# A scale moved behind the second layer's input projections

## The chip, the cores and the metric

One of the eight cores of a Trainium2 chip. The metric is the device time of one execution, in microseconds (us), and the number quoted is the median of repeated executions. Engines: TensorE (PE, with its weight loads shown apart as PEld), VectorE (DVE), ScalarE (ACT), GpSimd (POOL), and SyncE (SP), which issues the weight DMAs.

## The reference

Two transformer layers on 256 tokens (plus 16 meta tokens in the first), width 1024, in fp32. What surrounds the change is the end of layer 1 and the start of layer 2:

```python
        h = h + (jax.nn.silu(a @ w_gate[i]) * (a @ w_up[i])) @ w_down[i]

    h = rmsnorm(h, final_norm)
    return h[:, N_META:N_META + s_len]
...
    h = x
    for i in range(DEPTH):
        u = rms_norm(h, norm1_g[i])
        p_rwkv, p_nsa = jnp.split(u @ w_in[i], [N_RWKV_COLS], axis=-1)
        y_rwkv = rwkv7_time_mix(p_rwkv, ...)
        y_nsa = nsa_attention(p_nsa, ...)
```

So two norms follow each other with nothing between them: y = h * rsqrt(mean(h^2) + eps) * g3, and u = y * rsqrt(mean(y^2) + eps) * g4. Then 25 tiles of 128 projected features are made from u, of which 14 also get the time shift p + mu * (p_prev - p) before they are used.

## The kernel before

Activations lie feature-major: 8 tiles (k = 0 to 7) of 128 features by 256 tokens. Every fp32 product of activations with weights is made from three fp32r products: the operands are split into a rounded part (`hi`, by ACT) and a rest (`lo`, by DVE), and `part_products` (L536, matmuls on L539 to L541) adds hi*hi, hi*lo and lo*hi. Weights come in blocks of two tiles (1 MB) into a ring of two; for tile t, ACT's `split_hi` (L1382) writes `w_hi` and DVE's `split_lo` (L1851) writes `w_lo`, into 4 slots. `split_hi(t + 4)` can't start before tile t has been used up.

Each engine runs its own list of instructions in order, written out by hand; semaphores order them against each other (`wait_ge(name, n)` waits until the n-th instruction that signals the name is done).

**The end of layer 1.** The last two of the 22 down products run together, so that the 8 output tiles f come ready one after the other (`last_downs`). `add_down` (L2106) adds each to the residual `res`.

**The two norms.** With r = 1/sqrt(mean(h^2) + eps), both norms together scale a token by one factor, 1/sqrt(mean((g3^2 + eps) h^2) + eps^2). ACT squares each residual tile times sqrt(g3^2 + eps) (L1601), PE sums over features with 8 products with a matrix of ones into bank 3 (L864, fp32, each recorded as two passes), ACT makes the root (L1611, L1612), and DVE writes `act_in = res * (g3 g4) * root` (L2123), which ACT rounds (L1391) and DVE subtracts (L1859). Only then does tile 0 of the projections start. The plain squares, for r, are made by ACT (L1605) and summed by 8 further products in bank 2 (L869): five before tile 0, three between its products. r scales the residual later, off the path (L2200).

**The 25 projections.** PE's loop (from L980) makes tile t in bank t % 2: 24 matmuls. Before tile t it waits for the split of its weights and for tile t - 2 to have been read. Between the tiles PE does the small products of the two mixers: `decay_and_rate` before tile 3, `gates` before tile 4, `turn_values` before 6 and 12, key sums before 14 and 16, and for each of 8 attention units u: `nsa_scores` before tile 7 + 2u, `nsa_turn` (L960) before 10 + 2u and `nsa_values` (L975) before 11 + 2u.

A tile is read as follows. Plain tiles (2 to 10, 23, 24): ACT copies it out of the bank (L1680, L1682), and signals `proj2_plain`. Shifted tiles (0, 1 and 11 to 22): ACT writes mu * tile into `shift_buf` (L1677), and DVE adds the rest (L2182), and signals `shifted`. In its iteration t ACT then does `split_hi(t + 4)`, and, for odd t, the exponentials of unit (t - 7) / 2 (L1647) and the copy of the turned weights of unit (t - 9) / 2 (L1655), which `nsa_values` waits for. DVE in its iteration t does `split_lo(t + 4)`, for even t `nsa_kept` (L2160 to L2170) and `nsa_maxima` (L2150), and single steps such as L2200 (t = 5, 7, 9, 11), the key sums (13, 15), L2211 (15), L2215 and L2218 (17), L2221 and L2225 (19).

Layer 1's projections (L1968) read each tile with one DVE instruction that also scales it.

Of the kernel before, what the change touches and what calls it, by code (L numbers as in the profile page):

```python
# [13 lines left out]
P = 128  # L14
# [7 lines left out]
D = 1024  # L22
# [156 lines left out]
def constant_tables():  # L179
# [5 lines left out]
    c["eps_twice"] = np.full((P, 1), EPS * EPS)  # L185
# [82 lines left out]
def build_program(nc, xT, weights, consts, vecs, out):  # L268
# [14 lines left out]
    with ctx:  # L283
# [11 lines left out]
        gain_eps = sb("gain_eps", [P, KT])  # L295
# [42 lines left out]
        sq_gained = flat[:, 0:KT * SEQ].rearrange("p (k t) -> p k t", k=KT)  # L338
        sq_plain = flat[:, KT * SEQ:2 * KT * SEQ].rearrange("p (k t) -> p k t", k=KT)
# [195 lines left out]
        def _(pe):  # L535
# [326 lines left out]
            for k in range(KT):  # L862
                pe.wait_ge(S("norm_squares"), (nth("norm3") - 1) * KT + k + 1)
                mm = pe.matmul(ps[:, 3, 0:SEQ], C("ones"), sq_gained[:, k, :], start=(k == 0), stop=(k == KT - 1))  # L864
            mm.then_inc(S("norm_sums"), 1)

            def plain_sum(k):
                pe.wait_ge(S("plain_squares"), k + 1)
                mm = pe.matmul(ps[:, 2, 0:SEQ], C("ones"), sq_plain[:, k, :], start=(k == 0), stop=(k == KT - 1),  # L869
                               skip_group_check=True)  # L870
                if k == KT - 1:
                    mm.then_inc(S("plain_sums"), 1)

            for k in range(5):
                plain_sum(k)

# [103 lines left out]
            for t in range(TILES2):  # L980
                if t == 3:
                    decay_and_rate()
                if t == 4:
                    gates()
# [20 lines left out]
                if t >= 2:  # L1005
                    if is_shifted(t - 2):
                        pe.wait_ge(S("shifted"), shifted_upto(t - 2))
                    else:
                        pe.wait_ge(S("proj2_plain"), plain_upto(t - 2))
                if t == 0:  # L1010

                    for k in range(KT):
                        pe.wait_ge(S("normed"), normed("norm4", k))
                        mm = part_products(ps[:, 0, 0:SEQ], T_IN2 % SLOTS, k, act_hi[:, k, 0:SEQ], act_lo[:, k, 0:SEQ],
                                           k == 0, k == KT - 1)
                        if k == KT - 1:
                            mm.then_inc(S("proj2_ready"), 1)
                        if 2 <= k < 5:
                            plain_sum(k + 3)
                else:  # L1020
                    tile_products(ps[:, t % 2, 0:SEQ], (T_IN2 + t) % SLOTS, SEQ).then_inc(S("proj2_ready"), 1)
# [41 lines left out]
            pe.wait_ge(S("proj2_plain"), plain_upto(TILES2 - 1))  # L1063
# [286 lines left out]
        def _(act):  # L1350
# [245 lines left out]
            act.wait_ge(S("gains_squared"), 1)  # L1596
            step(act.activation(gain_eps[:], gain_eps[:], ACT.Ln, bias=C("eps")))
            step(act.activation(gain_eps[:], gain_eps[:], ACT.Exp, scale=0.5))
# [5 lines left out]
            def plain_square(k):  # L1604
                act.activation(sq_plain[:, k, :], res[:, k, META:CTX], ACT.Square).then_inc(S("plain_squares"), 1)  # L1605

            split_hi(T_IN2 + SLOTS - 2)
            for k in range(5):
                plain_square(k)
            act.wait_ge(S("norm_sums"), nth("norm3"))  # L1610
            step(act.activation(nrm[:, 0, 0:SEQ], ps[:, 3, 0:SEQ], ACT.Ln, bias=C("eps_twice"), scale=1.0 / D))  # L1611
            act.activation(nrm[:, 0, 0:SEQ], nrm[:, 0, 0:SEQ], ACT.Exp, scale=-0.5).then_inc(S("norm_root"), 1)  # L1612
            split_hi(T_IN2 + SLOTS - 1)
            for k in range(KT):
                round_tiles(0, SEQ, act_in, (k,))
                if k < 3:
                    plain_square(5 + k)
            act.wait_ge(S("plain_sums"), 1)
            step(act.activation(nrm[:, 1, 0:SEQ], ps[:, 2, 0:SEQ], ACT.Ln, bias=C("eps"), scale=1.0 / D))
            act.activation(nrm[:, 1, 0:SEQ], nrm[:, 1, 0:SEQ], ACT.Exp, scale=-0.5).then_inc(S("norm3_root"), 1)  # L1620
# [9 lines left out]
            def gather_blocks(x):  # L1630
                act.wait_ge(S("proj2_plain"), plain_upto((KC0, VC0)[x]))
# [39 lines left out]
            for t in range(TILES2):  # L1671
                act.wait_ge(S("proj2_ready"), t + 1)
                if is_shifted(t):
                    k = shifted_upto(t) - 1
                    if k >= 2:
                        act.wait_ge(S("shifted"), k - 1)
                    act.activation(shift_buf[:, k % 2, 1:1 + SEQ], ps[:, t % 2, 0:SEQ], ACT.Copy, scale=V("mu", k))\  # L1677
                        .then_inc(S("shift_scaled"), 1)
                elif t == GL0:
                    act.activation(proj2[0:24, t, :], ps[0:24, t % 2, 0:SEQ], ACT.Sigmoid).then_inc(S("proj2_plain"), 1)  # L1680
                else:
                    act.activation(proj2[:, t, :], ps[:, t % 2, 0:SEQ], ACT.Copy,  # L1682
                                   scale=HD ** -0.5 if Q0 <= t < Q0 + 4 else 1.0).then_inc(S("proj2_plain"), 1)
# [9 lines left out]
                if t == 2:  # L1693
# [6 lines left out]
                if t == 3:  # L1700
# [143 lines left out]
        def _(dve):  # L1844
# [258 lines left out]
            def add_down(layer, t):  # L2103
# [7 lines left out]
            dve.tensor_tensor(gain34[:], V("norm3", 0, KT), V("norm4", 0, KT), ALU.mult)  # L2111
            dve.tensor_tensor(gain_eps[:], V("norm3", 0, KT), V("norm3", 0, KT), ALU.mult)\
                .then_inc(S("gains_squared"), 1)
            for t in range(KT):
                add_down(1, t)


            split_lo(T_IN2 + SLOTS - 2)
            split_lo(T_IN2 + SLOTS - 1)
            dve.wait_ge(S("norm_root"), nth("norm3"))  # L2120
            for k in range(KT + 1):
                if k < KT:
                    dve.scalar_tensor_tensor(act_in[:, k, 0:SEQ], res[:, k, META:CTX], gain34[:, k:k + 1],  # L2123
                                             nrm[:, 0, 0:SEQ], ALU.mult, ALU.mult).then_inc(S("act_full"), 1)
                if k > 0:
                    rest("norm4", k - 1, SEQ, act_in)

# [50 lines left out]
            for t in range(TILES2):  # L2178
                if is_shifted(t):
                    k = shifted_upto(t) - 1  # L2180
                    dve.wait_ge(S("shift_scaled"), k + 1)
                    dve.scalar_tensor_tensor(proj2[:, t, :], ps[:, t % 2, 0:SEQ], om_mu[:, k:k + 1],  # L2182
                                             shift_buf[:, k % 2, 0:SEQ], ALU.mult, ALU.add).then_inc(S("shifted"), 1)
                if t + SLOTS < TILES2:
                    split_lo(T_IN2 + t + SLOTS)

                if t == 3:
# [360 lines left out]
```

## Time and profile before

| what | value |
|---|---|
| device time, median of 3 | 769.53 us (768.79 to 775.48) |
| the profiled execution: its own time | 774.36 us |
| its span (first to last record) | 772.6 us |
| its mean granted TensorE clock | 0.985 of full |
| busy: PE, DVE, ACT | 743.2, 503.7, 414.4 us |
| last down product of layer 1 starts | 351.11 us |
| tile 0 and tile 1 of the second projections start | 359.46, 365.42 us |
| first product behind the projections starts | 464.10 us |

A row of the timeline says when an instruction started, how long it took, and in brackets how long its engine sat idle before it and whose end released it. Rows can stand for several instructions in a row (xN). Consecutive instructions of one engine overlap a little, so that the distance between two starts is the cost in a queue, and the duration is what a waiting engine sees. Of the records of a matmul some are missing now and then.

### The profile page before, as it was taken

The numbers are of one execution on the slowest core, as the hardware profiler recorded it, in microseconds if no ns is written. First come the engines' busy times: TensorE is split into PE (matmuls) and PEld (weight loads), VectorE is DVE, ScalarE is ACT, GpSimd is POOL, SyncE is SP. The second block draws the span as 40 slices with busy tenths as digits, with TensorE's granted clock in tenths as the row PEclk, the third lists the DMA queues.
The fourth block names the chain that finished last, engine by engine and source line by source line (L and its number), as shares of the span: only waits on it lengthen the run. The fifth ranks groups of instructions, "written<-read, shape, count | busy, mean of one in ns | idle before, by whom it ended". The sixth has DMA issues, their size and how long they took to land.

```text
span 772.6 us, 16370 instructions
## 1 busy us (share of the span) xinstructions
PE 743.2 (96%) x6606; PEld 671.8 (87%) x6606; DVE 503.7 (65%) x913; ACT 414.4 (54%) x734; POOL 5.6 (1%) x13
## 2 busy tenths in 40 slices
PE   6999998999999999998999999989999999999996
PEld 5878786998888889997999998888898888889995
DVE  4655454668899994446566865444478999996445
ACT  5544544475666664337786662223367666665332
POOL 0000000000000000001000000000000000000000
PEclk9999999999999999999999999989999999999999
DMA  6622231336666454543343332301144645455431
GB/s 225 223 101 99 76 109 61 108 127 250 222 245 217 170 210 169 195 179 109 110 165 109 110 111 110 112 3 58 56 165 164 218 164 207 173 197 184 176 149 55
DMA packets 16740, 113.82 MB, mean 147 GB/s; under 512 B 2000, under 2 KB 2128, under 8 KB 3632
## 3 DMA queue, kind: packets, MB, share of 16 engines
q1 hardware_dynamic: 15984, 109.22, 39.7%
q0 software_dynamic: 704, 3.85, 1.5%
q8 instruction: 40, 0.66, 0.4%
q14 instruction: 12, 0.10, 0.0%
HBM read 112.01 MB, written 1.05 MB: 146 GB/s over the span
## 4 chain that ended last, share of the span: by engine, by line
PE 91%; DVE 4%; ACT 3%; issue 1%; DMA 1%; SPq 0%; DVEq 0%
PE ps L554 21%; PE ps L539 13%; PE ps L541 12%; PE ps L540 12%; PE ps L556 11%; PE ps L893 6%; PE ps L975 2%; DVE w_lo L1851 1%; PE ps L1031 1%; PE ps L855 1%; PE ps L721 1%; PE ps L960 1%; ACT w_hi L1382 1%; DMA vec<-in_vecs 1%; PE ps L933 0%
## 5 line engine op out<-in xcount | busy, mean ns | idle before, releaser
L1851 DVE TENSOR_TENSOR w_lo<-ring,w_hi 128x1024 fp32r<-128x1024 f32 x194 | 237.1, 1223 | 126.8 <-ACT w_hi L1382 125.6
L1382 ACT ACTIVATE w_hi<-ring 128x1024 fp32r<-128x1024 f32 x194 | 204.0, 1054 | 121.5 <-PE ps L541 110.7
L554 PE MATMUL ps<-acts,w_hi 128*128 128x512 f32 x704 | 246.2, 393 | 0.0
L556 PE MATMUL ps<-acts,w_lo 128*128 128x256 f32 x704 | 197.5, 281 | 0.0
L554 PEld LDWEIGHTS ps<-acts,w_hi 128*128 128x128 f32 x704 | 132.2, 188 | 29.5
L539 PE MATMUL ps<-acts,w_hi 128*128 128x256 f32 (+1 forms) x464 | 140.4, 303 | 6.2 <-DVE acts L1859 2.5
L541 PE MATMUL ps<-acts,w_lo 128*128 128x256 f32 (+1 forms) x464 | 133.7, 288 | 0.0
L540 PE MATMUL ps<-acts,w_hi 128*128 128x256 f32 (+1 forms) x464 | 133.6, 288 | 0.0
L556 PEld LDWEIGHTS ps<-acts,w_lo 128*128 128x128 f32 x704 | 132.4, 188 | 0.1
L539 PEld LDWEIGHTS ps<-acts,w_hi 128*128 128x128 f32 x464 | 89.5, 193 | 13.8 <-issue 7.3
L541 PE MATMUL ps<-hid_hi,w_lo 128*128 (+1 forms) x352 | 99.7, 283 | 0.0
L539 PE MATMUL ps<-hid_hi,w_hi 128*128 (+1 forms) x352 | 99.7, 283 | 0.0
L540 PE MATMUL ps<-hid_lo,w_hi 128*128 (+1 forms) x352 | 99.7, 283 | 0.0
L540 PEld LDWEIGHTS ps<-acts,w_hi 128*128 128x128 f32 x464 | 89.6, 193 | 1.2 <-issue 1.0
L541 PEld LDWEIGHTS ps<-acts,w_lo 128*128 128x128 f32 x464 | 89.6, 193 | 0.0
L539 PEld LDWEIGHTS ps<-hid_hi,w_hi 128*128 128x128 f32 x352 | 67.6, 192 | 0.1
L541 PEld LDWEIGHTS ps<-hid_hi,w_lo 128*128 128x128 f32 x352 | 67.6, 192 | 0.0
L540 PEld LDWEIGHTS ps<-hid_lo,w_hi 128*128 128x128 f32 x352 | 67.6, 192 | 0.0
L1968 DVE SCALAR_TENSOR_TENSOR arena<-ps,nrm 128x272 f32<-128x272 f32 (+1 forms) x21 | 9.1, 436 | 37.3 <-PE ps L541 37.3
L1574 ACT ACTIVATE hid_hi<-f 128x256 f32 (+1 forms) x44 | 18.4, 419 | 27.5 <-DVE f L2078 27.5
L1567 ACT ACTIVATE yT<-ps 128x256 f32<-128x256 f32 x44 | 16.6, 378 | 26.1 <-PE ps L556 26.0
L1562 ACT ACTIVATE yT<-ps 128x256 f32<-128x256 f32 x44 | 16.7, 379 | 21.2 <-PE ps L556 21.0
(344 smaller groups left out, 921.8 us busy)
## 6 DMA issues: line engine op xcount, KB each, us to landing
ring<-in_weights SPq DMA_DIRECT2D x101, 1024.0 KB, 4.8
res<-in_xT SPq DMA_DIRECT2D x2, 544.0 KB, 4.2
ring<-in_weights SPq DMA_DIRECT2D x2, 512.0 KB, 4.8
cst<-in_consts POOLq DMA_DIRECT2D x1, 1024.0 KB, 5.2
out_features<-yT SPq DMA_DIRECT2D x4, 256.0 KB, 2.2
cst<-in_consts POOLq DMA_DIRECT2D x1, 945.5 KB, 4.9
vec<-in_vecs POOLq DMA_DIRECT2D x1, 677.0 KB, 4.1
cst<-in_consts POOLq DMA_DIRECT2D x1, 656.0 KB, 5.2
```

Source lines behind the costliest of these rows:

```text
L539: pe.matmul(dst, w_hi[:, slot, k, :], hi, start=first, stop=False, skip_group_check=True)
L540: pe.matmul(dst, w_hi[:, slot, k, :], lo, start=False, stop=False, skip_group_check=True)
L541: return pe.matmul(dst, w_lo[:, slot, k, :], hi, start=False, stop=last, skip_group_check=True)
L554: pe.matmul(ps[:, bank, :].rearrange("p (x t) -> p x t", x=2), w_hi[:, slot, k, :], acts[:, :, at, 0:SEQ], start=(k == 0), stop=(k == KT - ...
L556: return pe.matmul(ps[:, bank, 0:SEQ], w_lo[:, slot, k, :], act_hi[:, at, 0:SEQ], start=False, stop=(k == KT - 1), skip_group_check=True)
L893: mm = pe.matmul(ps[hs, bank, cs], lhs(c, j)[hs], rhs(c, j, hs), start=start and (stop or (at == 0 and j == 0)), stop=stop, skip_group_che ...
L975: mm = pe.matmul(dst, pt_nsa[:, g, w0:w0 + P], vt_nsa[:, br, kt, grp(g)], start=(kt == 0), stop=(kt == t), skip_group_check=True)
L1382: act.activation(w_hi[:, t % SLOTS].rearrange("p k c -> p (k c)"), ring[:, b % RING, half].rearrange("p k c -> p (k c)"), ACT.Copy)\
L1562: act.activation(cross[:, m, 0, :], ps[:, 2 * m, SEQ:2 * SEQ], ACT.Copy).then_inc(S("gate_crossed"), 1)
L1567: act.activation(cross[:, m, 1, :], ps[:, 2 * m + 1, SEQ:2 * SEQ], ACT.Copy).then_inc(S("up_crossed"), 1)
L1574: act.activation(dst, sig2[:, m, :], ACT.Copy).then_inc(S("hid_rounded"), 1)
L1851: dve.tensor_tensor(w_lo[:, t % SLOTS].rearrange("p k c -> p (k c)"), ring[:, b % RING, half].rearrange("p k c -> p (k c)"), w_hi[:, t % S ...
```

## The change

The projections are made from `res * (g3 g4)` without the per-token factor, split while the down outputs are added; the factor is applied by DVE as it reads each projected tile.

- DVE makes a weight matrix `both_sums` (columns 0 to 63: g3^2 + eps, columns 64 to 127: ones) with a memset and a tensor_scalar, ahead of the additions. One set of 8 products gives both sums: rows 0 to 63 of bank 3 the gained one, rows 64 to 127 the plain one.
- For each k in turn: DVE adds, ACT rounds `res * gain`, DVE subtracts; ACT also squares.
- PE: tile 0, then the 8 sums, then tile 1. Then each of the two roots is spread over all 128 rows by one product of one row of ones. ACT copies both out of PSUM.
- Every tile is read by DVE (`proj2_taken`), which scales it. In shifted tiles ACT then makes mu * tile from SBUF, and DVE adds; ACT's copies of plain tiles are gone.
- Tiles 0, 1, 2 go to banks 1, 0, 6. Tile t waits for the reads up to t - 2. `decay_and_rate`, `gates`, their sigmoids, copies and the scan move one tile later.

```diff
+def bank2(t):
+
+    return {0: 1, 1: 0, 2: 6}.get(t, t % 2)
...
@@ PE @@
             for t in range(TILES2):
-                if t == 3:
+                if t == 4:
+
+                    pe.wait_ge(S("norm3_root"), 1)
                     decay_and_rate()
-                if t == 4:
+                if t == 5:
+                    pe.wait_ge(S("proj2_taken"), 3)
                     gates()
...
-                if t >= 2:
-                    if is_shifted(t - 2):
-                        pe.wait_ge(S("shifted"), shifted_upto(t - 2))
-                    else:
-                        pe.wait_ge(S("proj2_plain"), plain_upto(t - 2))
+                if t >= 3:
+                    pe.wait_ge(S("proj2_taken"), t - 1)
                 if t == 0:
 
                     for k in range(KT):
                         pe.wait_ge(S("normed"), normed("norm4", k))
...
+                    mm.then_inc(S("proj2_ready"), 1)
+                    pe.wait_ge(S("sums_weighted"), 1)
+                    for k in range(KT):
+                        pe.wait_ge(S("norm_squares"), (nth("norm3") - 1) * KT + k + 1)
+                        mm = pe.matmul(ps[:, 3, 0:SEQ], both_sums[:, k, :], sq[:, k, 0:SEQ], start=(k == 0),
+                                       stop=(k == KT - 1))
+                    mm.then_inc(S("norm_sums"), 1)
...
+                if t == 1:
+
+                    pe.wait_ge(S("norm_root"), nth("norm3"))
+                    for n in range(2):
+                        row = slice(HD * n, HD * n + 1)
+                        pe.matmul(ps[:, 3 - n, 0:SEQ], C("ones")[row, :], nrm[row, 0, 0:SEQ], start=True, stop=True)\
+                            .then_inc(S("scales_spread"), 1)
...
@@ ACT @@
+            act.wait_ge(S("gains_made"), 1)
             for k in range(KT):
                 act.wait_ge(S("down_added"), k + 1)
-                act.activation(sq_gained[:, k, :], res[:, k, META:CTX], ACT.Square, scale=gain_eps[:, k:k + 1])\
-                    .then_inc(S("norm_squares"), 1)
...
+                act.activation(act_hi[:, k, 0:SEQ], res[:, k, META:CTX], ACT.Copy, scale=gain34[:, k:k + 1])\
+                    .then_inc(S("act_rounded"), 1)
+                act.activation(sq[:, k, 0:SEQ], res[:, k, META:CTX], ACT.Square).then_inc(S("norm_squares"), 1)
             split_hi(T_IN2 + SLOTS - 2)
...
+            split_hi(T_IN2 + SLOTS - 1)
             act.wait_ge(S("norm_sums"), nth("norm3"))
...
             act.activation(nrm[:, 0, 0:SEQ], nrm[:, 0, 0:SEQ], ACT.Exp, scale=-0.5).then_inc(S("norm_root"), 1)
...
+            act.wait_ge(S("scales_spread"), 1)
+            act.activation(nrm[:, 1, 0:SEQ], ps[:, 3, 0:SEQ], ACT.Copy).then_inc(S("norm34_root"), 1)
+            act.wait_ge(S("scales_spread"), 2)
+            act.activation(nrm[:, 0, 0:SEQ], ps[:, 2, 0:SEQ], ACT.Copy).then_inc(S("norm3_root"), 1)
             act.preload_act_table_set("sigmoid_and_others")
...
             for t in range(TILES2):
-                act.wait_ge(S("proj2_ready"), t + 1)
                 if is_shifted(t):
                     k = shifted_upto(t) - 1
+                    act.wait_ge(S("proj2_taken"), t + 1)
                     if k >= 2:
                         act.wait_ge(S("shifted"), k - 1)
-                    act.activation(shift_buf[:, k % 2, 1:1 + SEQ], ps[:, t % 2, 0:SEQ], ACT.Copy, scale=V("mu", k))\
+                    act.activation(shift_buf[:, k % 2, 1:1 + SEQ], proj2[:, t, :], ACT.Copy, scale=V("mu", k))\
                         .then_inc(S("shift_scaled"), 1)
...
                 if t + SLOTS < TILES2:
                     split_hi(T_IN2 + t + SLOTS)
...
@@ DVE @@
+            dve.memset(both_sums[:, :, HD:P], 1.0)
+            dve.tensor_scalar(both_sums[:, :, 0:HD], gain_sq[:].unsqueeze(2).to_broadcast([P, KT, HD]), EPS, None,
+                              ALU.add).then_inc(S("sums_weighted"), 1)
+            dve.wait_ge(S("gains_made"), 1)
+            for k in range(KT):
+                add_down(1, k)
+                dve.wait_ge(S("act_rounded"), rounded("norm4", k))
+                dve.wait_ge(S("down_added"), k + 1)
+                dve.scalar_tensor_tensor(act_lo[:, k, 0:SEQ], res[:, k, META:CTX], gain34[:, k:k + 1],
+                                         act_hi[:, k, 0:SEQ].bitcast(F32), ALU.mult, ALU.subtract)\
+                    .then_inc(S("normed"), 1)
             split_lo(T_IN2 + SLOTS - 2)
             split_lo(T_IN2 + SLOTS - 1)
...
             for t in range(TILES2):
+
+                dve.wait_ge(S("proj2_ready"), t + 1)
+                if t == 0:
+                    dve.wait_ge(S("norm34_root"), 1)
+                n = 24 if t == GL0 else P
+                dve.scalar_tensor_tensor(proj2[0:n, t, :], ps[0:n, bank2(t), 0:SEQ], HD ** -0.5 if Q0 <= t < Q0 + 4 else 1.0,
+                                         nrm[0:n, 1, 0:SEQ], ALU.mult, ALU.mult).then_inc(S("proj2_taken"), 1)
+                if t + SLOTS < TILES2:
+                    split_lo(T_IN2 + t + SLOTS)
                 if is_shifted(t):
                     k = shifted_upto(t) - 1
                     dve.wait_ge(S("shift_scaled"), k + 1)
-                    dve.scalar_tensor_tensor(proj2[:, t, :], ps[:, t % 2, 0:SEQ], om_mu[:, k:k + 1],
+                    dve.scalar_tensor_tensor(proj2[:, t, :], proj2[:, t, :], om_mu[:, k:k + 1],
                                              shift_buf[:, k % 2, 0:SEQ], ALU.mult, ALU.add).then_inc(S("shifted"), 1)
-                if t + SLOTS < TILES2:
-                    split_lo(T_IN2 + t + SLOTS)
```

## Rows read from the trace of the kernel before

**Rows 1.** The page: shares of the chain that ended last, by engine.

```profile
PE 91%; DVE 4%; ACT 3%; issue 1%; DMA 1%; SPq 0%; DVEq 0%
```

**Rows 2.** Timeline of PE, 351 to 366 us: start us, us, line, operation, count [idle before, releaser].

```profile
351.11 0.28 PE L541 MATMUL ps<-hid_hi,w_lo 128*128 128x256 f32 x1
351.23 3.62 PE L864 MATMUL ps<-scratch,cst 128*128 128x256 f32 x16
354.68 2.32 PE L869 MATMUL ps<-scratch,cst 128*128 128x256 f32 x10
359.46 0.36 PE L539 MATMUL ps<-acts,w_hi 128*128 128x256 f32 x1 [2.46 <-DVE acts L1859]
...
365.42 0.28 PE L539 MATMUL ps<-acts,w_hi 128*128 128x256 f32 x1
```

**Rows 3.** Timeline of DVE, then of ACT, 347 to 367 us, same columns.

```profile
347.98 0.16 DVE L2112 TENSOR_TENSOR gain_eps<-vec 128x8 f32<-128x8 f32 x1
348.06 1.41 DVE L2106 TENSOR_TENSOR res<-ps,res 128x256 f32<-128x256 f32 x4
...
358.88 0.43 DVE L1859 TENSOR_TENSOR acts<-act_in,acts 128x256 fp32r<-128x256 f32 x1
359.23 0.48 DVE L2123 SCALAR_TENSOR_TENSOR act_in<-res,gain,nrm 128x256 f32<-128x256 f32 x1
...
358.44 0.42 ACT L1391 ACTIVATE acts<-act_in 128x256 fp32r<-128x256 f32 x1 [1.69 <-DVE act_in L2123]
...
365.52 1.28 ACT L1621 ACT_TABLE_LOAD   x1
```

**Rows 4.** Single operations by line: count, duration ns min/median/max, first and last start.

```profile
L1601 ACT ACTIVATE scratch<-res,gain_eps x8: 493/496/512, 348.7 to 351.9; 128x256 f32<-128x256 f32 x8
...
L1982 DVE MEMSET arena<- x1: 285/285/285, 32.7 to 32.7; 6x272 f32 x1
...
L2175 DVE TENSOR_SCALAR scratch<-ps x2: 685/685/685, 418.0 to 427.6; 128x512 f32<-128x512 f32 x2
```

**Rows 5.** Busy time by stretch: PE, PEld, DVE, ACT, POOL, granted clock, DMA.

```profile
360.40:361.40 1.00, 1.00 (x5) 0.98 (x5) 1.00 (x4) 0.68 (x3) 0.00 (x0) 0.50 0.99 418
...
363.40:364.40 1.00, 1.00 (x8) 0.92 (x7) 0.81 (x5) 0.41 (x1) 0.07 (x1) 1.00 0.00 0
19.00:21.00 2.00, 0.36 (x3) 0.14 (x2) 2.00 (x4) 2.00 (x3) 1.21 (x2) 1.00 0.00 0
22.00:24.00 2.00, 2.00 (x11) 2.00 (x10) 1.63 (x3) 0.00 (x0) 0.00 (x0) 0.50 1.02 405
502.00:504.00 2.00, 0.80 (x28) 0.66 (x24) 0.64 (x1) 1.13 (x3) 0.00 (x0) 1.00 0.04 8
```

**Rows 6.** Timeline of DVE, 407 to 439 us, in the second half of the projections.

```profile
407.92 1.23 DVE L1851 TENSOR_TENSOR w_lo<-ring,w_hi 128x1024 fp32r<-128x1024 f32 x1 [0.46 <-ACT w_hi L1382]
409.06 0.88 DVE L2200 SCALAR_TENSOR_TENSOR res<-res,vec,nrm 128x256 f32<-128x256 f32 x2
...
413.48 0.17 DVE L2160 RECIPROCAL cst<-cst 128x4 f32<-128x4 f32 x1
...
415.93 0.48 DVE L2182 SCALAR_TENSOR_TENSOR arena<-ps,cst,arena 128x256 f32<-128x256 f32 x1
...
437.15 1.67 DVE L2215 SCALAR_TENSOR_TENSOR arena<-arena,cst,scratch 128x256 f32<-128x256 f32 x4
```

**Rows 7.** Timeline of ACT, 406 to 453 us.

```profile
406.47 0.47 ACT L1677 ACTIVATE arena<-ps,vec 128x256 f32<-128x256 f32 x1 [1.80 <-PE ps L541]
406.84 1.05 ACT L1382 ACTIVATE w_hi<-ring 128x1024 fp32r<-128x1024 f32 x1
...
446.37 0.79 ACT L1655 ACTIVATE arena<-ps 128x768 f32<-128x768 f32 x1
...
452.02 0.48 ACT L1677 ACTIVATE arena<-ps,vec 128x256 f32<-128x256 f32 x1 [3.56 <-PE ps L541]
```

**Rows 8.** Timeline of PE, value products of one unit.

```profile
447.54 1.55 PE L975 MATMUL ps<-arena 128*128 128x64 f32 x12
```

More of the change, by code:

```diff
@@ L184, in constant_tables @@
     c["eps"] = np.full((P, 1), EPS)
-    c["eps_twice"] = np.full((P, 1), EPS * EPS)
+    c["eps_halves"] = np.where(i[:, None] < HD, EPS * EPS, EPS)
     c["one"] = np.ones((P, 1))
@@ L860, in _ @@
             feed_forward(1, T_UP1)
[L862 to L875, printed above, removed]
             def chunk_of(x, c, j):
@@ L926, in turn_values @@
                 if with_gates:
+                    pe.wait_ge(S("branch_gates"), 1)
                     for t in range(2):
@@ L1594, in _ @@
             feed_forward(1, T_UP1)
-            act.wait_ge(S("gains_squared"), 1)
-            step(act.activation(gain_eps[:], gain_eps[:], ACT.Ln, bias=C("eps")))
-            step(act.activation(gain_eps[:], gain_eps[:], ACT.Exp, scale=0.5))
+            act.wait_ge(S("gains_made"), 1)
             for k in range(KT):
                 act.wait_ge(S("down_added"), k + 1)
-                act.activation(sq_gained[:, k, :], res[:, k, META:CTX], ACT.Square, scale=gain_eps[:, k:k + 1])\
-                    .then_inc(S("norm_squares"), 1)
-            def plain_square(k):
-                act.activation(sq_plain[:, k, :], res[:, k, META:CTX], ACT.Square).then_inc(S("plain_squares"), 1)
+                act.activation(act_hi[:, k, 0:SEQ], res[:, k, META:CTX], ACT.Copy, scale=gain34[:, k:k + 1])\
+                    .then_inc(S("act_rounded"), 1)
+                act.activation(sq[:, k, 0:SEQ], res[:, k, META:CTX], ACT.Square).then_inc(S("norm_squares"), 1)
             split_hi(T_IN2 + SLOTS - 2)
-            for k in range(5):
-                plain_square(k)
+            split_hi(T_IN2 + SLOTS - 1)
             act.wait_ge(S("norm_sums"), nth("norm3"))
-            step(act.activation(nrm[:, 0, 0:SEQ], ps[:, 3, 0:SEQ], ACT.Ln, bias=C("eps_twice"), scale=1.0 / D))
+            step(act.activation(nrm[:, 0, 0:SEQ], ps[:, 3, 0:SEQ], ACT.Ln, bias=C("eps_halves"), scale=1.0 / D))
             act.activation(nrm[:, 0, 0:SEQ], nrm[:, 0, 0:SEQ], ACT.Exp, scale=-0.5).then_inc(S("norm_root"), 1)
[L1613 to L1620, printed above, removed]
+            act.wait_ge(S("scales_spread"), 1)
+            act.activation(nrm[:, 1, 0:SEQ], ps[:, 3, 0:SEQ], ACT.Copy).then_inc(S("norm34_root"), 1)
+            act.wait_ge(S("scales_spread"), 2)
+            act.activation(nrm[:, 0, 0:SEQ], ps[:, 2, 0:SEQ], ACT.Copy).then_inc(S("norm3_root"), 1)
             act.preload_act_table_set("sigmoid_and_others")
@@ L2110, in _ @@
             feed_forward(1, T_UP1)
[L2111 to L2115, printed above, removed]
+            dve.tensor_tensor(gain34[:], V("norm3", 0, KT), V("norm4", 0, KT), ALU.mult).then_inc(S("gains_made"), 1)
+            step(dve.tensor_tensor(gain_sq[:], V("norm3", 0, KT), V("norm3", 0, KT), ALU.mult))
+            dve.memset(both_sums[:, :, HD:P], 1.0)
[9 more added lines that the diff above has]
+                    .then_inc(S("normed"), 1)
             split_lo(T_IN2 + SLOTS - 2)
             split_lo(T_IN2 + SLOTS - 1)
[L2120 to L2126, printed above, removed]
             dve.wait_ge(S("normed"), normed("norm4", KT - 1))
```

39 lines of the change are left out of this document (15 added, 24 removed).

## The prediction

> **What bounds the kernel now.** I read the chain of waits first: 91% of what ended last is PE [rows 1]. So a change counts only where PE stands still, runs at the lower clock, or gets or loses instructions. The next view is PE's timeline around the norms [rows 2]. Layer 1's last down product starts at 351.11, tile 1 of the projections at 365.42, so 14.3 us lie between, of which tile 0 itself is 24 matmuls at the 0.12 us between 351.11 and 351.23, or 2.86. The 8 gained sums take 3.45 (351.23 to 354.68, 0.216 for each of 16 passes), the 8 plain ones as much, and the rest is a 2.46 wait and the lower clock behind it: TensorE is granted 0.50 of full, the 1.2 GHz level, in 360.4 to 361.4, and 1.00 again from 363.4 [rows 5]. The timelines of DVE and ACT [rows 3] show what PE waits for: root, scale, round, subtract. Behind tile 1 PE goes on while DVE and ACT alternate beside it, each often waiting for the other [rows 6, 7]; the change touches what they do there, so I read these rows as closely as the norms.
>
> **The first stretch, norms and tile 0.** Removed from it: 8 plain sums on PE and the root ahead of tile 0. But DVE now handles each output by a full round trip, since its queue is in order: the addition k + 1 stands behind the subtraction k, and that waits for ACT's rounding k. One round: addition 0.42 (four take 1.41 [rows 3]), 0.03 to hand over, ACT's copy with a gain per row 0.50 (the same form, L1601 [rows 4]), 0.02 back (358.44 + 0.42 to 358.88 [rows 3]), subtraction 0.40 to the next start (0.48 less the 0.08 by which neighbours overlap). That is 1.37 us, and 8 of them 11.0. Squares lie in ACT's gaps and cost nothing.
>
> The rounds also start later. The small products end at about 348.2; then come the memset and the tensor_scalar of 512 elements, before the first addition, which started at 348.06. No row shows either at this size. A memset of 272 elements took 0.285, so 512 at its rate take 0.54; a tensor_scalar of 512 from PSUM took 0.685 [rows 4]. Bounds for both together: 0.3, if each costs no more than half the small memset, and 1.6, if both cost more than the PSUM form; I take 1.0, by these two rows, and the additions start at 349.2. The last subtraction starts at 349.2 + 7 x 1.37 + 0.97 = 359.8 and ends at 360.3, tile 0 ends at 360.7. PE has 0.36 of work in each 1.37 until then.
>
> Then the 8 sums: 3.45 at full clock, 6.9 at half. In before, PE idled for 2.5 us and had the lower clock until some 4 us after it went on; here it is still three quarters of the time for 9 us. I take the lower clock for the first half of the sums, 5.2 in all, so tile 1 starts at 365.9: **+0.5**, with ends of -1.3 (full clock, early start) and +2.8 (half clock for all, late start). So the 3.45 saved on PE is given back by the round trips.
>
> **Spreading the roots.** Two products of 256 columns behind tile 1, 2 passes each: **+0.9** on PE (4 x 0.216 [rows 2]). Bounds: 0.4 and 1.7.
>
> **A new wait before tile 3.** Tile 1 ends at 368.75, the first spread product some 0.45 later, and ACT's copy (0.4, by 358.44 [rows 3]) at 369.7. DVE reads tile 0. ACT makes its second copy (370.1), loads its table, 1.28 [rows 3] (371.4), writes mu * tile 0 (0.4) and splits the weights, 1.08 until DVE can follow (406.84 to 407.92 [rows 6, 7]): 372.9. DVE's split takes 1.14 (407.92 to 409.06 [rows 6]), the shifted tile 0.40, then it reads tile 1: 374.9. PE is through with tile 2 at 369.6 + 2.86 = 372.5 and needs tile 1's bank, for which nothing is left between (the lora products moved behind tile 3): **+2.4**. Bounds: 0, if the table load lies elsewhere and DVE is 1.1 faster, and 4. Lora products, gates and scan move, and cost what they did. Banks 2 and 3 are free of the roots by then. SP loads the weights of tiles 6 and 7 once those of tile 3 are split, some 5 us later than before, and ACT wants them 10 us after that; the load stays covered.
>
> **Tiles 3 to 10** are plain. DVE gets 0.40 for each, ACT loses as much; `split_hi` doesn't wait for the read, so the DVE splits have their weights when the read is done. A pair costs DVE 2 x (0.40 + 1.14) + 2.45 + 0.8 = 6.3 us, PE more than 7. Nothing: **0**.
>
> **Tiles 11 to 20** are where it is decided. ACT's order is mu * tile, then `split_hi(t + 4)`; DVE's is read, `split_lo(t + 4)`, shifted tile. Before, ACT took the tile from the bank, so DVE had only the last two. Now ACT waits for DVE's read and DVE for ACT's split, in each tile: read to ACT 0.51; 0.37 to the split (406.47 to 406.84 [rows 7]); 1.08 to DVE's split; 1.14; shifted tile 0.40. That is 3.50 per tile. Ten tiles: 35.0. The even ones also have `nsa_kept` and `nsa_maxima`, 2.45 (413.48 to 415.93 [rows 6]): 5 x 2.45 = 12.2. Single steps: two L2200 0.80, two key sums 1.22, L2211 1.22, L2215 and L2218 2.95 (437.15, five instructions [rows 6]), L2221 and L2225 2.26: 8.45. So DVE needs 55.7 from its read of tile 11 to that of tile 21. PE went from the end of tile 11 (ACT's copy at 406.47) to that of tile 21 (452.02) in 45.55 [rows 7]. Could DVE lag without PE noticing? The unit's weights are ready at 446.37 + 0.79 = 447.16 and PE's value products begin at 447.54 [rows 7, 8]: 0.38 of slack, and the read puts 0.51 in front of it. So a lag reaches PE one for one, by `nsa_values`: 55.7 - 45.55 = **+10.1**. Bounds: +1, if each tile costs 0.9 less than these queue distances say, and +14, if ACT's exponentials are in the way too.
>
> **Sum.** 0.5 + 0.9 + 2.4 + 0 + 10.1 = 13.9 us. The profiled execution took 774.36 (span 772.6 and 1.8 around it) and would take 788.3; that execution is 4.8 above the median, so against the median of 769.53 I forecast **783.4 us**. The stages behind, of the same instructions in the same order, start later by this and keep their length.
>
> **Rivals.**
>
> *The late waits also cost the clock.* After PE's gap of 19 to 21 the clock was 0.50 in 22 to 24, after the 2.46 wait too; yet in 502 to 504 PE was busy for 0.80 of 2.00 and kept 1.00 [rows 5]. The new waits are of 2.4 before tile 3 and some 2 to 3.5 in each of the later pairs, with full work behind. A fall lasts about 3.6 us (359.8 to 363.4) and loses half, 1.8. Where DVE sets the pace a slower PE costs little; two falls on the path give +3.6, 787.0. The Trainium skill warns of just this in "TensorE: Matmul & The Clock Gate", section "A second HAM failure mode: psum-queue depth-cycling": PE that idles briefly but often between groups of matmuls can go back and forth between its clock levels. By that rule the first stretch too, with its gap of a microsecond per output, would be low throughout, as I took it.
>
> *The pace holds.* If the alternation in tiles 11 to 20 costs no more than PE's 9.1 per pair, only the first three terms are left, +3.8: 773.3. For it: DVE is idle for a good third of the span. Against it: that idle time is made of waits for ACT, which become longer.
>
> *DVE's queue is not held by ACT, the other side.* If DVE's additions ran ahead of ACT's rounding, tile 0 would run with the last down outputs. The place is the round per output; it decides from a round of 0.72 (6 matmuls of 0.12, an output's pace on PE) downwards, and in the pairs from 9.1. Tile 1 would start at 351.23 + 2.86 + 3.45 = 357.5, 7.9 earlier; with the spread that is -7.0: 762.5. Against it: the order in the diff, and the rows add to 1.37.
>
> **Chances.** The forecast 0.58 (777.5 to 786), clock falls 0.20, pace holds 0.14, unheld queue 0.08. A measurement tells about 1% (7.7 us) from no change. Slower by more: the first two, 0.78. Within 1%: pace holds and half of the last, 0.18. Faster by over 1%: 0.04, the last with a bit more than its price. The range takes in "pace holds" from below with 1 us of room, and the clock falls with 3 above: 772.5 to 790.
>
> **What would show it.** First stretch: DVE's additions some 1.37 apart and not in groups; PE's first 8 triples as far apart; granted clock 0.50 in the sums; tile 1 near 366. Then a PE gap of over 2 us ahead of tile 3, released by DVE's read; a distance of about 1.6 us between DVE's read and its split in shifted tiles; 55 us from the read of tile 11 to that of tile 21; PE idle before the value products of units 3 to 7, released by ACT's weights. The forecast is wrong if the rounds are under a microsecond, or DVE reads tiles 13 to 21 within 0.5 us of their end.

## The result and the profile after

The changed kernel takes 788.4 us (median of 4, 786.24 to 789.08); the kernel before, run beside it on the same chip, 772.5 (768.79 to 775.92). The ratio is 1.0202, 95% interval 1.0137 to 1.0266: slower, by 1.4 to 2.7 per cent. The profiled execution took 789.08, its span is 787.3 against 772.6. The median of before lay at 769.5 to 772.9 in the groups of runs of this study, so kernels are compared below by ratios within a group, and traces by distances, since an execution that happens to have more low clock than another is longer at places that the edit doesn't touch.

The page first, shares of the chain that ended last, by engine:

```profile
PE 82%; DVE 9%; ACT 5%; issue 2%; DMA 1%; SPq 0%; DVEq 0%; ACTq 0%
```

PE had 91% of it [rows 1]: DVE and ACT have come onto the path. The stretch ahead of tile 1, timeline of PE:

```profile
351.46 0.28 PE L541 MATMUL ps<-hid_hi,w_lo 128*128 128x256 f32 x1
351.58 0.28 PE L539 MATMUL ps<-acts,w_hi 128*128 128x256 f32 x1
...
353.73 0.39 PE L539 MATMUL ps<-acts,w_hi 128*128 128x256 f32 x1 [0.77 <-DVE acts L2105]
355.13 0.39 PE L539 MATMUL ps<-acts,w_hi 128*128 128x256 f32 x1 [0.78 <-DVE acts L2105]
...
360.71 0.58 PE L539 MATMUL ps<-acts,w_hi 128*128 128x256 f32 x1 [0.38 <-DVE acts L2105]
...
361.51 4.94 PE L1006 MATMUL ps<-act_in,scratch 128*128 128x256 f32 x16
366.11 0.47 PE L539 MATMUL ps<-acts,w_hi 128*128 128x256 f32 x1
```

The triples of tile 0 are 1.40 us apart, each released by DVE's subtraction. DVE in the same stretch:

```profile
348.67 0.48 DVE L2097 MEMSET scratch<- 128x512 f32 x1 [0.17 <-DVE gain_sq L2096]
349.07 0.36 DVE L2098 TENSOR_SCALAR scratch<-gain_sq 128x512 f32<-128x512 f32 x1
349.35 0.41 DVE L2090 TENSOR_TENSOR res<-ps,res 128x256 f32<-128x256 f32 x1
...
350.80 0.42 DVE L2090 TENSOR_TENSOR res<-ps,res 128x256 f32<-128x256 f32 x1
351.79 0.48 DVE L2105 SCALAR_TENSOR_TENSOR acts<-res,gain,acts 128x256 fp32r<-128x256 f32 x1 [0.58 <-ACT acts L1595]
352.19 0.42 DVE L2090 TENSOR_TENSOR res<-ps,res 128x256 f32<-128x256 f32 x1
```

In [rows 3] four additions stood together in 1.41 us; now each stands alone, behind a subtraction that idled 0.58 for ACT. Busy time by stretch shows what this does to PE. A row has the stretch, its length, the busy time of PE, PEld, DVE, ACT and POOL (with how many instructions), the granted clock, and the DMA's share and GB/s:

```profile
356.00:358.00 2.00, 0.70 (x4) 0.50 (x4) 1.42 (x4) 1.07 (x3) 0.00 (x0) 0.84 0.00 0
358.00:360.00 2.00, 1.62 (x6) 1.32 (x6) 1.02 (x3) 1.19 (x3) 0.00 (x0) 0.50 0.00 0
...
362.00:364.00 2.00, 2.00 (x6) 1.62 (x5) 2.00 (x6) 0.34 (x1) 0.86 (x1) 0.50 0.00 0
364.00:366.00 2.00, 2.00 (x10) 1.72 (x9) 0.02 (x1) 0.00 (x0) 0.00 (x0) 0.95 0.62 115
```

The rows at the two edges (0.84 and 0.95) put the lower level from 357.4 to 364.2, so the sums pay. Next, DVE and PE around the start of tile 3:

```profile
370.48 0.42 DVE L2164 SCALAR_TENSOR_TENSOR arena<-ps,nrm 128x256 f32<-128x256 f32 x1 [6.46 <-ACT nrm L1604]
373.42 1.23 DVE L1835 TENSOR_TENSOR w_lo<-ring,w_hi 128x1024 fp32r<-128x1024 f32 x1 [2.51 <-ACT w_hi L1378]
...
374.96 0.42 DVE L2164 SCALAR_TENSOR_TENSOR arena<-ps,nrm 128x256 f32<-128x256 f32 x1
```

```profile
375.52 0.35 PE L539 MATMUL ps<-acts,w_hi 128*128 128x256 f32 x1 [2.56 <-DVE arena L2164]
```

DVE reads tile 0, idles 2.51 for ACT, splits, and reads tile 1 only at 374.96. The second half of the projections, DVE's reads of tiles 11 and 21 and its first split between them, then ACT:

```profile
410.97 0.42 DVE L2164 SCALAR_TENSOR_TENSOR arena<-ps,nrm 128x256 f32<-128x256 f32 x1 [0.56 <-PE ps L541]
412.92 1.23 DVE L1835 TENSOR_TENSOR w_lo<-ring,w_hi 128x1024 fp32r<-128x1024 f32 x1 [1.52 <-ACT w_hi L1378]
...
466.00 0.42 DVE L2164 SCALAR_TENSOR_TENSOR arena<-ps,nrm 128x256 f32<-128x256 f32 x1
```

```profile
411.44 0.51 ACT L1663 ACTIVATE arena<-arena,vec 128x256 f32<-128x256 f32 x1 [2.64 <-DVE arena L2164]
411.85 1.04 ACT L1378 ACTIVATE w_hi<-ring 128x1024 fp32r<-128x1024 f32 x1
```

From read to read are 55.03 us, where ACT's copies of the same tiles were 45.55 apart [rows 7]. DVE waits for ACT's split once in each of the ten tiles, 1.52 to 1.71; ACT waits for DVE's read in eight of them, and in tiles 12 and 14 it is still busy when the read is done. (The prediction's sign of "about 1.6" between read and split fits this idling; from start to start it is 1.95, the 0.51 + 0.37 + 1.08 of its sum.) PE has only this to show: the view of its waits from 345 to 480 us (total, times, longest), the two longest of these waits, and the first product behind the projections:

```profile
PE ps L961 <- ACT arena L1641: 7.4, 5, 3.2
```

```profile
446.70 1.55 PE L961 MATMUL ps<-arena 128*128 128x64 f32 x12 [2.29 <-ACT arena L1641]
458.92 1.43 PE L961 MATMUL ps<-arena 128*128 128x64 f32 x9 [3.25 <-ACT arena L1641]
```

```profile
477.94 0.44 PE L1027 MATMUL ps<-arena,scratch 64*64 64x128 f32 x4 [0.52 <-DVE arena L2164]
```

The five waits are those of units 2 to 6, of 0.49, 0.34, 2.29, 3.25 and 1.05. The first product behind the projections started at 464.10 before: 13.84 later, of which 0.35 was there already at the last down product (351.46 against 351.11). The remaining 0.9 of the span's 14.7 comes behind it, where instructions and order are the same.

### The profile page after: what moved, and what is told of

The parts are those of the page before. It is cut to its first block, busy times and chain, and to the rows that moved or that the text cites. A ratio compares the mean times of both kernels' runs of the same rounds, so it can differ in the third digit from the quotient of the medians.

```text
span 787.3 us, 16356 instructions
## 1 busy us (share of the span) xinstructions
PE 746.1 (95%) x6594; PEld 672.3 (85%) x6594; DVE 509.8 (65%) x932; ACT 409.3 (52%) x714; POOL 5.6 (1%) x13
## 3 DMA queue, kind: packets, MB, share of 16 engines
HBM read 112.01 MB, written 1.05 MB: 144 GB/s over the span
## 4 chain that ended last, share of the span: by engine, by line
PE 82%; DVE 9%; ACT 5%; issue 2%; DMA 1%; SPq 0%; DVEq 0%; ACTq 0%
PE ps L554 21%; PE ps L539 11%; PE ps L556 11%; PE ps L541 11%; PE ps L540 10%; PE ps L878 6%; DVE w_lo L1835 2%; ACT w_hi L1378 2%; PE ps L1027 1%; PE ps L855 1%; PE ps L721 1%; DVE arena L2130 1%; ACT arena L1633 1%; PE ps L1006 1%; PE ps L961 1%
```

## The experiments

All times below that are called distances count from the start of layer 1's last down product in the same trace, and are read from PE's and DVE's timelines. The table holds all kernels; the text under each run uses it.

| kernel | tile 11 read | tile 11 to 21 | first product behind | ratio to before (95%) |
|---|---|---|---|---|
| before | 55.36 | 45.55 | 112.99 | 1 |
| after | 59.51 | 55.03 | 126.48 | 1.0202 (1.0137 to 1.0266) |
| e1, ACT splits first | 61.65 | 46.10 | 119.69 | 1.0082 (1.0056 to 1.0109) |
| e2, additions one ahead | 54.59 | 55.03 | 123.02 | 1.0139 (1.0087 to 1.0190) |
| e3, table load early | 59.43 | 55.04 | 126.39 | 1.0188 (1.0134 to 1.0242) |
| e5, reads by DVE alone | 55.55 | 55.02 | 124.08 | 1.0148 (1.0093 to 1.0203) |
| e4, e1 + e2 + e3 | 51.27 | 46.11 | 109.31 | 0.9960 (0.9935 to 0.9984) |
| e7, e4 and tile 4's split early | 50.31 | 46.11 | 108.35 | 0.9945 (0.9924 to 0.9967) |
| e8, shifted step first on DVE | 59.43 | 51.88 | 124.80 | 1.0155 (1.0113 to 1.0197) |
| e6, PE kept busy | 59.35 | 55.04 | 129.41 | 1.0183 (1.0142 to 1.0225) |

**e1: ACT splits the weights before it waits for the read.**

```diff
 for t in range(TILES2):
+    if t + SLOTS < TILES2:
+        split_hi(T_IN2 + t + SLOTS)
     if is_shifted(t):
         act.wait_ge(S("proj2_taken"), t + 1)
...
-    if t + SLOTS < TILES2:
-        split_hi(T_IN2 + t + SLOTS)
```

> The changed kernel, but ScalarE issues split_hi(t + 4) at the head of its iteration t, ahead of mu * tile, so DVE's split no longer waits for a ScalarE step that itself waits for DVE's read. DVE's work is the same, instruction for instruction. Theory (order: DVE and ScalarE wait for each other in every shifted tile): the distance from DVE's read to its split in shifted tiles falls from 1.94 us to under 1, the stretch from the read of tile 11 to that of tile 21 from 55.0 us to 45.5 to 47, the wait before tile 3 by 0.4 us, and the time by 8 to 10 us. Rival (load: DVE has 25 reads of 0.4 us more to do, 10 us, wherever they stand): the stretch stays within 1.5 us of 55, and the time falls by less than 2 us.

Measured: 777.76 us, ratio 1.0082, some 9 us less than the changed kernel. DVE in a shifted tile, read then split, and the read of tile 21:

```profile
413.61 0.42 DVE L2164 SCALAR_TENSOR_TENSOR arena<-ps,nrm 128x256 f32<-128x256 f32 x1 [0.56 <-PE ps L541]
414.71 1.23 DVE L1835 TENSOR_TENSOR w_lo<-ring,w_hi 128x1024 fp32r<-128x1024 f32 x1 [0.67 <-ACT w_hi L1378]
...
459.71 0.42 DVE L2164 SCALAR_TENSOR_TENSOR arena<-ps,nrm 128x256 f32<-128x256 f32 x1
```

DVE idles 0.67 instead of 1.52, the ten tiles take 46.10 instead of 55.03, and none of PE's waits at the value products reaches a microsecond. Not one instruction was added or taken away: the 9 us are the order in ACT's queue. The edit leaves 0.55 over the 45.55 of before. (The traced execution took 785.87, the longest of eleven with a median of 777.76. Its tile 11 is later than the changed kernel's because it had more low clock, in 356.5 to 366.7 and again in 377.0 to 380.4 behind tile 3's wait; so only its ten tiles are compared here, and its 119.69 in the table is too late for the kernel as a rule.)

**e5: the reads alone**, put into the kernel before: DVE takes every tile out of the bank (times 1, or the query scale), ACT makes mu * tile from SBUF, in the order of the change. Norms and first stretch stay as before.

```diff
+dve.wait_ge(S("proj2_ready"), t + 1)
+dve.tensor_scalar(proj2[0:n, t, :], ps[0:n, t % 2, 0:SEQ], HD ** -0.5 if Q0 <= t < Q0 + 4 else 1.0,
+                  None, ALU.mult).then_inc(S("proj2_taken"), 1)
...
```

> One part alone, put into the kernel before: the norms, the sums, the order of the small products and the scaled input of the projections are as before, but DVE reads each tile out of its bank (a tensor_scalar), ScalarE makes mu * tile from SBUF behind that read, and its plain copies are gone. Theory (order in the shifted tiles): 9 to 10.5 us slower than before, all of it between tile 11 and tile 21, where the distance goes from 45.6 to about 55 us; tile 3 starts at most 1 us later than before, since the lora products lie before it. Rival (the stretch is only tight because the norms and the scan come later in the changed kernel): 0 to 3 us slower.

Measured: 785.53, ratio 1.0148, 11.4 us above before.

```profile
406.80 0.42 DVE L2177 TENSOR_SCALAR arena<-ps 128x256 f32<-128x256 f32 x1 [0.56 <-PE ps L541]
408.74 1.23 DVE L1847 TENSOR_TENSOR w_lo<-ring,w_hi 128x1024 fp32r<-128x1024 f32 x1 [1.52 <-ACT w_hi L1380]
...
461.82 0.42 DVE L2177 TENSOR_SCALAR arena<-ps 128x256 f32<-128x256 f32 x1
```

55.02 us, and the same 1.52 of idling: with the norms of before, the alternation is there at its full price. The first product behind comes 11.09 later than before: 9.47 of it in the ten tiles, 0.19 ahead of them, and 1.43 from tile 21 on (13.51 instead of 12.08), where the clock was low from 466.1 to 469.5.

**e8: the same wait attacked on DVE's side.** The shifted step stands ahead of `split_lo`.

```diff
-if t + SLOTS < TILES2:
-    split_lo(T_IN2 + t + SLOTS)
 if is_shifted(t):
     k = shifted_upto(t) - 1
     dve.wait_ge(S("shift_scaled"), k + 1)
...
+if t + SLOTS < TILES2:
+    split_lo(T_IN2 + t + SLOTS)
```

> The changed kernel with one change on DVE alone: the shifted tile's step ahead of split_lo. The alternation theory: in each of the ten shifted tiles the step fills DVE's wait for ACT's split, so that read to read costs 0.51 + 0.37 + 1.08 + 1.14 = 3.10 instead of 3.50 us; ten tiles give 4.0, the read of tile 11 to that of tile 21 takes 51 instead of 55.03 us, and the median is about 784.5. The rival, that DVE's amount of work sets the pace: the same instructions are there, so 55 us and 788.

Measured: 784.48, ratio 1.0155, and 51.88 us for the ten tiles; so the amount of DVE's work isn't what sets the pace. The saving is 3.15, not 4.0. That the median met the 784.5 is chance: the ratio's interval overlaps that of the changed kernel, and the first product behind comes only 1.68 earlier, since the clock was low from 465.1 to 468.5. DVE in tiles 11 and 12:

```profile
409.71 0.49 DVE L2169 SCALAR_TENSOR_TENSOR arena<-arena,cst 128x256 f32<-128x256 f32 x1 [0.58 <-ACT arena L1663]
410.65 1.23 DVE L1835 TENSOR_TENSOR w_lo<-ring,w_hi 128x1024 fp32r<-128x1024 f32 x1 [0.46 <-ACT w_hi L1378]
...
414.17 0.48 DVE L2169 SCALAR_TENSOR_TENSOR arena<-arena,cst 128x256 f32<-128x256 f32 x1 [1.17 <-ACT arena L1663]
```

In tile 11 the step fills the wait, and the read of tile 12 comes 3.89 behind that of tile 11 instead of 4.28. In tile 12 DVE then waits 1.17 for mu * tile: ACT is still at the exponentials and the weights' copy of the odd iteration, and what DVE gained is lost again. I had taken ACT to be free at each read.

**e2: DVE's additions one output ahead of its subtractions.**

```diff
+add_down(1, 0)
 for k in range(KT):
-    add_down(1, k)
+    if k + 1 < KT:
+        add_down(1, k + 1)
     dve.wait_ge(S("act_rounded"), rounded("norm4", k))
```

> The changed kernel, but DVE adds down output k + 1 before it waits for ScalarE's rounding of k. Theory (the first stretch is set by the round trip of 1.40 us per output): the rounds become 0.75 to 0.85 us, the last subtraction ends near 356.5 instead of 360.65 us, the 8 sums run at full clock or nearly (3.5 to 4.5 us instead of 4.6), tile 1 starts near 361 instead of 366.1, and the time falls by 4.5 to 6 us, since nothing behind it depends on when it began. Rival (the stretch behind absorbs it, as DVE's pace there is set by something with a fixed time, such as the weight loads): the time falls by less than 2 us, with longer waits behind.

Measured: 783.27, ratio 1.0139, about 5 us less by the ratios, whose intervals overlap; the distances below are the firmer evidence. DVE, a round; then PE's sums and tile 3:

```profile
351.24 0.42 DVE L2090 TENSOR_TENSOR res<-ps,res 128x256 f32<-128x256 f32 x1
351.57 0.47 DVE L2107 SCALAR_TENSOR_TENSOR acts<-res,gain,acts 128x256 fp32r<-128x256 f32 x1
351.97 0.41 DVE L2090 TENSOR_TENSOR res<-ps,res 128x256 f32<-128x256 f32 x1
```

```profile
356.13 3.61 PE L1006 MATMUL ps<-act_in,scratch 128*128 128x256 f32 x16
...
368.78 0.36 PE L539 MATMUL ps<-acts,w_hi 128*128 128x256 f32 x1 [2.56 <-DVE arena L2166]
```

A round takes 0.73 instead of 1.40, the sums run at full clock, and tile 1 starts at 359.39 (361 was expected), and tile 3 at a distance of 17.60 instead of 24.06: 6.5 earlier. But the wait before tile 3 stays at 2.56, and this time the clock falls behind it:

```profile
370.00:374.00 4.00, 4.00 (x22) 3.69 (x22) 2.41 (x4) 2.31 (x5) 0.00 (x0) 0.57 0.43 104
```

So tile 11 gains only 4.9 of the 6.5, and another fall, at 465.7 to 469.1, takes 1.5 behind tile 21 (13.40 instead of 11.94). The first product behind gains 3.5.

**e3: the table load ahead of the two copies**, where ACT waits for PE anyway.

```diff
 act.activation(nrm[:, 0, 0:SEQ], nrm[:, 0, 0:SEQ], ACT.Exp, scale=-0.5).then_inc(S("norm_root"), 1)
+act.preload_act_table_set("sigmoid_and_others")
 act.wait_ge(S("scales_spread"), 1)
...
-act.preload_act_table_set("sigmoid_and_others")
```

> The changed kernel, but ScalarE loads its sigmoid table directly behind the root, in the 2.5 us in which it waits for the spread products, and not behind the two copies. Theory (the table load stands in the chain that ends in the wait before tile 3): the wait before tile 3 falls from 2.56 to 1.3 us and the time by 1.3. Rival (the wait is set by DVE's split of tile 4's weights, whose ScalarE half could be late for its own reasons): the wait changes by less than 0.4 us.

Measured: 788.07, ratio 1.0188: a gain that this measurement can't tell from none. Its trace shows the edit at work, and where it went:

```profile
360.14 5.82 PE L1006 MATMUL ps<-act_in,scratch 128*128 128x256 f32 x16
...
374.07 0.36 PE L539 MATMUL ps<-acts,w_hi 128*128 128x256 f32 x1 [1.63 <-DVE arena L2164]
```

The wait fell from 2.56 to 1.63, not to the 1.3 expected, since ACT now idles 0.38 for DVE's read of tile 0, which the table load had covered. But in this execution the clock had fallen one round earlier (a triple at 355.15 already takes 0.58 for its first product), and the sums took 5.47 instead of 4.60. The gain of 0.9 stands in the wait and is too small for the total to show.

**e4: all three edits together.**

> The three edits of e1, e2 and e3 together: ACT's split of the next weights ahead of mu * tile, DVE's additions one output ahead, the table load ahead of the copies. If their places are separate, the parts add up. Counted from layer 1's last down product, the first product behind the projections starts 126.5 us later in the changed kernel, 113.0 in the kernel before; with e2's 6.5 for the first stretch, e3's 0.9 and e1's 8.9 for the pairs that is about 110 to 112.8 (the upper end if the clock falls that e2 showed at 370 and 464 stay). Forecast 0 to 3 us below the kernel before, ratio 0.996 to 1.000. The rival, that one wait takes the place of another and the parts don't add: no better than e1 alone, ratio 1.005 to 1.009.

Measured: 769.36, ratio 0.9960 (0.9935 to 0.9984), slightly under before. The first product behind has the distance 109.31, 3.7 less than before. From the changed kernel it is 17.17 earlier, where the three edits had taken 6.8 (8.9 in the ten tiles of e1's long execution), 3.5 and 0.1 off that distance one by one. The parts add up, and more: no fall of the clock is left between 352 and 470.

```profile
368.00 0.36 PE L539 MATMUL ps<-acts,w_hi 128*128 128x256 f32 x1 [0.73 <-DVE arena L2166]
```

The wait before tile 3 is 0.73 with all three edits, and the clock after it is 1.00.

**e7: e4 with tile 4's weights split behind tile 3's**, in the time in which PE makes the sums.

```diff
 split_hi(T_IN2 + SLOTS - 1)
+split_hi(T_IN2 + SLOTS)
...
-    if t + SLOTS < TILES2:
+    if 0 < t < TILES2 - SLOTS:
         split_hi(T_IN2 + t + SLOTS)
```

(and the same on DVE with `split_lo`).

> e4 with tile 4's weights split right behind tile 3's, while PE makes the sums. If the wait before tile 3 is the chain copy of the root, ACT's split, DVE's split, read of tile 1, it loses its two splits, 1.04 + 1.14 us: DVE reads tile 1 about 1.4 us behind its read of tile 0, before PE is through with tile 2, and the wait is under 0.3 us, with no clock fall behind it. First product behind the projections 1.2 to 2.7 us earlier than in e4; ratio to the kernel before 0.993 to 0.997. The rival, that the wait moves one tile on (the split of tile 5 is then the late one, before tile 4): a wait of over 1 us before tile 4 and no gain over e4.

Measured: 768.93, ratio 0.9945 (0.9924 to 0.9967), the fastest of all kernels here. PE has no wait before tile 3 or 4. DVE's reads of tiles 0 and 1, and PE behind the projections:

```profile
361.70 0.42 DVE L2168 SCALAR_TENSOR_TENSOR arena<-ps,nrm 128x256 f32<-128x256 f32 x1 [3.51 <-ACT nrm L1606]
...
363.17 0.42 DVE L2168 SCALAR_TENSOR_TENSOR arena<-ps,nrm 128x256 f32<-128x256 f32 x1
```

```profile
457.47 0.33 PE L1027 MATMUL ps<-arena,scratch 64*64 64x128 f32 x2 [0.52 <-DVE arena L2168]
```

Tile 1 is read 1.47 behind tile 0, as expected. The gain over e4 is 0.96 in distance, under the 1.2 to 2.7 expected, since in e4 the wait was already down to 0.73 and had cost no clock. The totals of e4 and e7 can't be told apart.

**e6: is the lower clock in the sums due to PE's idling?** Six further products, into a bank nobody reads, behind each of the first seven triples of tile 0.

```diff
+if k < KT - 1:
+    for n in range(2):
+        part_products(ps[:, 3, 0:SEQ], T_IN2 % SLOTS, k, act_hi[:, k, 0:SEQ], act_lo[:, k, 0:SEQ], True, True)
```

> The changed kernel with six further products behind each of PE's first seven triples of tile 0, into a bank nobody reads, so that PE is busy for 1.08 of each 1.40 us instead of 0.36. If the lower clock in the sums comes from PE's idling in the rounds, the granted clock stays at 1.00 from 352 to 366, the 16 passes of the sums take 3.5 instead of 4.94 us, and tile 1 starts 13.1 to 13.3 us behind layer 1's last down product instead of 14.65: 1.3 to 1.5 us earlier, median about 787. The rival, that the clock falls there for another reason (a transfer, ACT's and DVE's work): 0.50 in the sums as before and no gain.

```profile
358.00:360.00 2.00, 1.85 (x13) 1.66 (x14) 1.14 (x3) 1.06 (x3) 0.00 (x0) 1.00 0.00 0
...
362.00:364.00 2.00, 2.00 (x11) 1.77 (x10) 2.00 (x6) 0.46 (x1) 0.95 (x1) 1.00 0.00 0
```

```profile
361.28 3.61 PE L1010 MATMUL ps<-act_in,scratch 128*128 128x256 f32 x16
364.55 0.47 PE L539 MATMUL ps<-acts,w_hi 128*128 128x256 f32 x1
```

Measured: the clock holds at 1.00, the sums take 3.61, and tile 1 starts at a distance of 12.97 instead of 14.65: the idling it was. The total (787.19, ratio 1.0183) is 1.5 below the changed kernel in ratio, within the interval, and the trace shows that little of it is left: the wait of 2.56 before tile 3 was now followed by a fall of the clock (0.61 in 374 to 376, 0.54 in 376 to 378), and tile 11 is read 0.16 earlier, not 1.7. A further fall, at 470.0 to 476.8, makes the first product behind 2.93 later than in the changed kernel.

## Why the prediction was right, and where it was off

The forecast was +13.9 us; the profiled executions differ by 14.7, and the ratio of 1.0202 is 15.6 us on 772.5, with an interval of 10.6 to 20.5. In the profiled execution's own scale the forecast was 788.3, and that one took 789.08. As a median, the forecast was 783.4 and 788.4 came: 3.0 of the 5.0 are the base, which stood at 769.53 as the median of three runs and is 772.5 of four, and 2.0 are the change. By its number alone 788.4 lies above the band of the forecast (777.5 to 786), where the rival of the clock falls had its place (787.0); it is the trace, and not the number, that tells them apart. The sum also came near partly by chance: of the 14.7, 0.35 was there before the change begins and 0.86 came behind it, and the terms themselves make 13.49 of 13.9, with misses both ways. Term by term:

*First stretch, forecast +0.5.* Measured 14.65 from the last down product to tile 1 against 14.31: +0.34. The rounds were taken at 1.37 and are 1.40. Memset and tensor_scalar were taken at 1.0 and cost 0.68 from the first's start to the first addition, with 0.17 of idling ahead; they began later than taken, so the additions start at 349.35 instead of 349.2. The sums took 4.60 (361.51 to 366.11), taken at 5.2: the clock was low until 364.2, and had come down at 357.4, in the fourth gap of some 0.78, not from the start. e2 shows what "unheld queue" priced: a round of 0.73 as named there, but tile 1 at a distance of 8.21, where the rival had 6.4 (its sums were to start at 354.1, and start at 356.13). Its rounds were possible all along; only the order forbade them.

*Spread, forecast +0.9.* Its four passes take 0.72 between the last triple of tile 1 and tile 2 (369.14 to 369.86).

*The wait before tile 3, forecast +2.4.* Measured 2.56, by the chain that was worked out. e3 and e1 take pieces of that chain away (0.93 and 0.40), and e7, on top of the other edits, all that is left, so this step is shown and not only argued.

*Tiles 3 to 10, forecast 0.* Tile 11 is read 4.15 later (59.51 against 55.36), of which the terms above give 3.62; 0.5 stays unexplained. It lies ahead of tile 6, whose first product is already 4.16 later (37.03 against 32.87), so for tiles 6 to 10 the 0 holds.

*Tiles 11 to 20, forecast +10.1.* Measured +9.48. 55.7 were forecast from read to read, 55.03 came. e5 has it with nothing else of the change, e1 takes 8.93 of it away by order alone, e8 3.15 from the other side. PE's slack ahead of the value products can be read off the lags. The reads of tiles 13, 15, 17, 19 and 21 lag by 1.29, 1.69, 3.23, 6.72 and 9.48 more than that of tile 11. The value products that wait for ACT's copies of these iterations (units 2 to 6) lag by 0.62, 1.03, 3.38, 6.87 and 9.63 more than those before tile 11. So there was some 0.66 of slack at units 2 and 3, where 0.38 was taken, and from unit 4 on the lag reaches PE whole; the first product behind has 13.49 of 13.63. (The prediction named units 3 to 7 for PE's waits; they were 2 to 6, one of them, unit 6, behind the ten tiles.)

*The stages behind, forecast to keep their length.* They took 0.9 more. In this study that part's length varies by some us from trace to trace with its falls of the clock, so nothing of it is put down to the change.

The rival "the late waits also cost the clock" did not come true at its first place in the changed kernel: after the 2.56 wait the clock stayed at 1.00, and the one fall behind a late wait (459.8 to 463.2, after 3.25 of waiting) lies where DVE sets the pace: the ten tiles took 55.03, as in e2 and e6 (55.03 and 55.04), whose clock was low there for 6.8 instead of 3.4. In e2 and e6 a fall did follow the wait before tile 3. That a wait is the cause of such a fall is argued from their order in time; only for the rounds does a run show it (e6). The Trainium skill's section "A second HAM failure mode: psum-queue depth-cycling" of "TensorE: Matmul & The Clock Gate" says that short, frequent idling between groups of matmuls can send the clock back and forth between its levels. The rounds agree, with 0.50 from 357.4 on and 1.00 in e6 where the gaps are filled; but the prediction's reading of it, low throughout the first stretch, is more than the section says, and the trace has 1.00 in the first rounds. The rival "the pace holds" falls with e5.

What the forecast missed is the other half of the picture: with both orders, the table load and tile 4's split mended, the same idea is worth about half a per cent (e7). Two orders in the queues cost some 14 us, taken one at a time (9 by e1, 5 by e2), and hid what the change as such, fewer sums and no root ahead of tile 0, may bring. How much of the half per cent is its own isn't shown: no run gives the kernel before an earlier table load or an earlier split of tile 4's weights.

## What to carry to other kernels

When a read moves from one engine to another, look at what stands behind that read in both queues. Work that doesn't need the read (here the split of the next weights) belongs ahead of the wait for it; here that order alone was worth 9 us of 770, with no instruction changed. Likewise, where an in-order engine makes both the input and the last step of a round trip through another engine, let it run one input ahead, which halved the round from 1.40 to 0.73; and judge gains below one per cent by distances in the trace, since the totals move as much with the clock.

## What the runs showed of the hardware that was not expected

Whether a wait of some 2 us brings the clock down is not settled by its length. Before the same tile 3, with the same full work behind, it fell after 2.56 in e2 and e6 and after 2.16 in e1, and stayed at 1.00 after 2.56 in the changed kernel, 1.63 in e3 and 2.16 in e8. In e2 and e6 PE had had the full clock all the way from layer 1, but e1 had been low until 366.7, as the changed kernel until 364.2. The waits ahead of the value products are as mixed: a fall right behind 2.33 in e2 (at 441.8), none behind 2.29 in the changed kernel (446.70) or 2.60 in e3 (468.03). So no rule comes out of these, and it stays open. What it means for the work: a gap closed at one place (e6) can bring the fall at the next, and of 1.7 us gained 0.16 were left. In e4 and e7, where the waits are at most 0.73, there was none from 352 to 470.

ACT's scaled pass over a 128x256 tile is no cheaper from SBUF than from the bank: 0.51 (L1663) against 0.47 in [rows 7]. So moving the bank's read to DVE saved ACT nothing in shifted tiles.
